# Two transformer blocks in fp32 on one core: low-part products one block later, weight conversions behind them, buffers for squares, and an earlier last split

## The reference

```python
def rms_norm(x, g):
    return x * lax.rsqrt(jnp.mean(x * x, axis=-1, keepdims=True) + EPS) * g

def first_block(x, p, ...):
    z = rms_norm(h, g_mix_pre) @ w_in            # D=1024
    ...                                          # convolution, attention, short convolution, pooling
    h = h + rms_norm(mix, g_mix_post)            # mix = concat(...) @ w_out
    ff = jnp.square(jax.nn.relu(rms_norm(h, g_mlp_pre) @ w_up)) @ w_down
    h = h + rms_norm(ff, g_mlp_post)
    gate = jax.nn.sigmoid(rms_norm(h, g_ple_pre) @ w_ple_gate)
    return h + rms_norm((p @ w_ple_proj) * gate, g_ple_post)

def second_block(x, ...):
    z = rmsnorm(x, ln_mix_g) @ w_in
    ...                                          # sliding attention, gated linear attention
    x = x + merged @ w_out
    a, u = jnp.split(rmsnorm(x, ln_ffn_g) @ w_ffn_in, 2, axis=-1)
    return x + (jax.nn.silu(causal_dwconv(a)) * u) @ w_ffn_out
```

## Time and profile before

| | us |
|---|---|
| median of 3 runs | 1488.1 |
| lowest and highest | 1486.35, 1490.41 |
| the profiled execution | 1486.49 |
| its span in the profile | 1484.7 |
| busy: TensorE, VectorE, ScalarE, GpSimd | 1454.5, 804.9, 560.2, 257.8 |
| mean granted clock of TensorE (1 is full) | 0.993 |

### The profile page before, as it was taken

One profiled execution on the slowest core, in us unless ns is written; L12 is line 12 of the kernel. 1 busy time (PEld: TensorE's weight loads), 2 busy tenths in 40 slices (PEclk: granted clock), 3 DMA queues, 4 the chain that ended last, 5 costly groups with the idle time before them and its releaser, 6 DMA issues.

```text
span 1484.7 us, 17752 instructions
## 1 busy us (share of the span) xinstructions
PE 1454.5 (98%) x6978; PEld 1188.2 (80%) x6978; DVE 804.9 (54%) x1167; ACT 560.2 (38%) x829; POOL 257.8 (17%) x170
## 2 busy tenths in 40 slices
PE   9999989999999999889999999999999999999998
PEld 7866768888888887767888888888887888888887
DVE  5688465433333347675767734734535665534554
ACT  5345434522324124442455546322224443323310
POOL 4234344301101012341033201300003000000000
PEclk9999999999999999999999999999999999999999
DMA  6221222333323332221211211233332233332331
GB/s 229 86 71 57 71 64 78 114 99 99 101 86 98 99 100 73 72 69 59 84 43 44 68 47 57 90 95 100 97 102 77 80 114 99 98 101 86 102 99 69
DMA packets 36131, 129.18 MB, mean 87 GB/s; under 512 B 4024, under 2 KB 4280, under 8 KB 36048
## 3 DMA queue, kind: packets, MB, share of 16 engines
q1 hardware_dynamic: 35760, 127.78, 27.6%
q10 hardware_dynamic: 288, 0.26, 0.1%
HBM read 125.91 MB, written 2.10 MB: 86 GB/s over the span
## 4 chain that ended last, share of the span: by engine, by line
PE 89%; DVE 5%; ACT 2%; issue 2%; POOL 1%; DMA 0%; ACTq 0%; DVEq 0%; POOLq 0%
PE P L1080 27%; PE P L1082 26%; PE P L1081 26%; PE P L1339 1%; DVE P L1893 1%; PE P L1225 1%; DVE WST L2125 1%; POOL AC L2370 1%; PE P L1121 1%; PE P L1176 1%; PE P L1301 1%; POOL DD L2370 1%; PE P L1382 0%; PE P L1322 0%; PE P L1187 0%
## 5 line engine op out<-in xcount | busy, mean ns | idle before, releaser
L1080 PE MATMUL P<-AH,WH 128*128 128x512 f32 x1104 | 444.9, 403 | 11.0 <-issue 5.0
L1082 PE MATMUL P<-AH,WL 128*128 128x512 f32 x1104 | 433.5, 393 | 0.0
L1081 PE MATMUL P<-AL,WH 128*128 128x512 f32 x1104 | 433.1, 392 | 0.0
L1419 ACT ACTIVATE WH<-WR 128x1024 fp32r<-128x1024 f32 x232 | 244.0, 1052 | 338.5 <-PE P L1082 322.6
L1739 DVE TENSOR_TENSOR WL<-WR,WH 128x1024 fp32r<-128x1024 f32 x215 | 277.1, 1289 | 148.8 <-ACT WH L1419 148.1
L1080 PEld LDWEIGHTS P<-AH,WH 128*128 128x128 f32 x1104 | 209.1, 189 | 64.4 <-issue 13.9
L1082 PEld LDWEIGHTS P<-AH,WL 128*128 128x128 f32 x1104 | 209.1, 189 | 44.8
L1081 PEld LDWEIGHTS P<-AL,WH 128*128 128x128 f32 x1104 | 209.5, 190 | 42.0 <-issue 0.7
L1080 PE MATMUL P<-FH,WH 128*128 128x512 f32 x432 | 168.0, 389 | 0.0
L1081 PE MATMUL P<-FL,WH 128*128 128x512 f32 x432 | 168.0, 389 | 0.0
L1082 PE MATMUL P<-FH,WL 128*128 128x512 f32 x432 | 168.0, 389 | 0.0
(11 more groups left out here) (323 smaller groups left out, 1867.7 us busy)
## 6 DMA issues: line engine op xcount, KB each, us to landing
WR<-in_ws SPq DMA_DIRECT2D x232, 512.0 KB, 3.6
out<-Y SPq DMA_DIRECT2D x8, 256.0 KB, 2.0
H<-in_xT SPq DMA_DIRECT2D x3, 512.0 KB, 7.8
C<-in_const SPq DMA_DIRECT2D x1, 946.5 KB, 10.6
H<-in_xT SPq DMA_DIRECT2D x2, 256.0 KB, 4.2
PR<-in_pT SPq DMA_DIRECT2D x1, 512.0 KB, 4.8
WR<-in_ws SPq DMA_DIRECT2D x1, 384.0 KB, 4.6
WR<-in_ws ACTq DMA_DIRECT2D x1, 128.0 KB, 3.8
```

Source lines behind the costliest of these rows:

```text
L1080: e.matmul(P, wh, xh, start=start, stop=False)
L1081: e.matmul(P, wh, xl, start=False, stop=False)
L1082: ins = e.matmul(P, wl, xh, start=False, stop=stop)
L1419: e.activation(m.WH[:, c % NW, :], m.WR[:, c % NRAW, :], ACT.Copy).then_inc(*at.up("w_hi", "w_hi", c))
```

## The change

It does six things. (1) In a head, the three matmuls of a block product are taken apart: `mm_hi` does `WH` with `AH` and `WL` with `AH` for block j of all tiles, then `mm_lo` does `WH` with `AL` of block j-1, so low parts lag one block; from the fourth chunk on, `ahead` is called at `mm_lo`. (2) Every head has five tiles side by side (the gate's had four), and `sums` stands in the middle of block 7. (3) In stage 5 the splits and squares of blocks 0 to 5 are said inside the loop of `mix2`. (4) At `p1` and `p3` squares 5 and 6 have buffers of their own, square 6 is added on VectorE, and one `warm` product goes. (5) The addition of `H` block 1 moves from GpSimd to VectorE. (6) The root's first guess takes one operation fewer.

```diff
@@ -312,31 +312,54 @@
             self.say("w_load", NRAW)
             make(1)
             self.say("square", s, 0, 0)
-        else:
+        elif s != "5":
             make(0)
             make(1)
             rest(0)
-        rest(1)
-        make(2)
-        got = [self.ring() for _ in range(3)] + [self.bank(b) for b in (6, 7)[:len(specs) - 4]]
+        if s != "5":
+            rest(1)
+            make(2)
+        got = [self.ring() for _ in range(3)] + [self.bank(b) for b in (6, 7)]
+        behind = []
+
+        def low(j):
+            for t, i in zip(got, behind):
+                if i // CH >= 3:
+                    self.ahead(i)
+                self.say("mm_lo", t, i, (x, j), j == 7)
         for j in range(8):
-            if j == 7:
-                self.sums(s, 0)
+            ids = []
             for m, t in enumerate(got):
-                self.block(t, specs[m][j], (x, j), j == 0, j == 7)
+                if j == 7 and m == 2:
+                    self.sums(s, 0)
+                i = len(self.plan)
+                if i // CH < 3:
+                    self.ahead(i)
+                self.plan.append(specs[m][j])
+                ids.append(i)
+                self.say("mm_hi", t, i, (x, j), j == 0)
+            if j:
+                low(j - 1)
+            behind = ids
+            if s == "5":
+                if j < 2:
+                    make(j + 6)
+                    rest(j + 6)
+                continue
             if j < 5:
                 make(j + 3)
             if j < 6:
                 rest(j + 2)
+        low(7)
         b = self.spread(s)
-        out = got + [self.tile(specs[len(got)], [(x, j) for j in range(8)])]
+        out = got + [self.tile(q, [(x, j) for j in range(8)]) for q in specs[5:]]
         self.say("rbc", s, b)
         return out
 
     def post(self, n, direct, fill=None):
 
         if fill is None:
-            self.say("warm", self.bank(6), 3)
+            self.say("warm", self.bank(6), 2)
         self.sums(n, direct)
         if fill is None:
             self.say("warm", self.bank(6), 2)
@@ -627,6 +650,10 @@
             t = self.tile([block("w_out_2", 128 * q, 128 * m) for q in range(8)], [("M2", q) for q in range(8)])
             self.say("mix2", m, t)
             self.close(t)
+            if 0 < m < 7:
+                self.say("x_hi", "5", m - 1)
+                self.say("x_lo", "5", m - 1)
+                self.say("square", "5", m - 1, 0)
         return lambda m: None
 
     def decay(self):
@@ -963,6 +990,13 @@
     def rs(self, i):
         return (self.RS, self.RT)[i // 4][:, i % 4, :]
 
+    def square(self, n, i):
+
+        SQ, AC = self.sq(n)
+        if n in ("p1", "p3") and i >= 5:
+            return SQ[:, 1, :] if i == 7 else self.post(n)[1][:, i - 5, :]
+        return AC if i == 0 else SQ[:, i % 2, :]
+
     def rbc(self, s):
         return {"1": self.RBC1, "2": self.RBC2, "3": self.RBC2, "4": self.RBC3, "5": self.RBC4}[s]
 
@@ -1080,6 +1114,31 @@
         e.matmul(P, wh, xh, start=start, stop=False)
         e.matmul(P, wh, xl, start=False, stop=False)
         ins = e.matmul(P, wl, xh, start=False, stop=stop)
+        if stop:
+            ins.then_inc(*at.up("full", "full", t.id))
+            if ends:
+                at.also(("full", t.id), "w_used", c)
+        elif ends:
+            ins.then_inc(*at.up("w_used", "w_used", c))
+
+    def mm_hi(t, i, x, start):
+
+        c, o = i // CH, (i % CH) * 128
+        P, xh = m.bank[t.bank][:], m.x(*x)[0]
+        part = int(o >= FIRST)
+        w.wait_ge(*(at("w_hi", c) if c else at("w_hi0", part)))
+        w.wait_ge(*at("x_hi", *x))
+        if start:
+            free(t)
+        e.matmul(P, m.WH[:, c % NW, o:o + 128], xh, start=start, stop=False)
+        w.wait_ge(*(at("w_lo", c) if c else at("w_lo0", part)))
+        e.matmul(P, m.WL[:, c % NW, o:o + 128], xh, start=False, stop=False)
+
+    def mm_lo(t, i, x, stop):
+
+        c, wh, wl, ends = weights(i)
+        w.wait_ge(*at("x_lo", *x))
+        ins = e.matmul(m.bank[t.bank][:], wh, m.x(*x)[1], start=False, stop=stop)
         if stop:
             ins.then_inc(*at.up("full", "full", t.id))
             if ends:
@@ -1162,7 +1221,7 @@
 
 
     def sums(n, t, direct):
-        SQ, AC = m.sq(n)
+        AC = m.sq(n)[1]
         if first[0]:
             first[0] = False
             w.wait_ge(*at("params"))
@@ -1178,7 +1237,7 @@
         if direct:
             w.wait_ge(*at("square", n, 7))
             for q in range(4):
-                ins = e.matmul(P[:, q:q + 1], SQ[:, 1, 128 * q:128 * q + 128], one, start=False, stop=True,
+                ins = e.matmul(P[:, q:q + 1], m.square(n, 7)[:, 128 * q:128 * q + 128], one, start=False, stop=True,
                                skip_group_check=True)
         ins.then_inc(*at.up("full", "full", t.id))
 
@@ -1434,11 +1493,12 @@
             *at.up("x_hi", "x_hi", "A" + s, i))
 
     def square(n, i, direct):
-        SQ, AC = m.sq(n)
         w.wait_ge(*at("summand", n, i))
-        if i >= 3:
+        if n in ("p1", "p3") and i >= 5:
+            w.wait_ge(*at("summed", n, 3))
+        elif i >= 3:
             w.wait_ge(*at("summed", n, i - 2))
-        e.activation(AC if i == 0 else SQ[:, i % 2, :], m.summed(n, i), ACT.Square).then_inc(
+        e.activation(m.square(n, i), m.summed(n, i), ACT.Square).then_inc(
             *at.up("square", "square", n, i))
 
 
@@ -1757,10 +1817,7 @@
         v, y, u = m.roots(name, n)
         e.tensor_scalar(v, ps, scale, EPS, ALU.mult, ALU.add).then_inc(*at.up("newton", "root0", name))
         w.wait_ge(*at("root0", name))
-        e.tensor_scalar(u.bitcast(I32), v.bitcast(I32), 1, None, ALU.logical_shift_right).then_inc(
-            *at.up("newton", "root1", name))
-        w.wait_ge(*at("root1", name))
-        e.tensor_scalar(y.bitcast(I32), u.bitcast(I32), -1.0, float(0x5F3759DF), ALU.mult, ALU.add).then_inc(
+        e.tensor_scalar(y.bitcast(I32), v.bitcast(I32), -0.5, float(0x5F3759DF), ALU.mult, ALU.add).then_inc(
             *at.up("newton", "root2", name))
         w.wait_ge(*at("root2", name))
         for k in range(3):
@@ -1777,6 +1834,14 @@
         rsqrt(n, m.bank[t.bank][:, 0:4], 4, 1.0 / 1024)
         at.also(("root0", n), "read", t.id)
 
+    def square(n, i, direct):
+
+        if n in ("p1", "p3") and i == 7:
+            AC = m.sq(n)[1]
+            w.wait_ge(*at("square", n, 6))
+            w.wait_ge(*at("summed", n, 5))
+            e.tensor_tensor(AC, AC, m.square(n, 6), ALU.add).then_inc(*at.up("summed_last", "summed", n, 6))
+
     def rbc(s, t):
         w.wait_ge(*at("full", t.id))
         e.tensor_copy(m.rbc(s)[:], m.bank[t.bank][:]).then_inc(*at.up("rbc", "rbc", s))
@@ -1794,7 +1859,7 @@
             *at.up("normed", "normed", n, i))
         if i == 7:
             at.also(("normed", n, 7), "read", t.id)
-        if i % 2 == 0:
+        if i % 2 == 0 or i == 1:
             w.wait_ge(*at("normed", n, i))
             e.tensor_tensor(m.H[:, i, :], m.H[:, i, :], u, ALU.add).then_inc(*at.up("h", "h", s, i))
 
@@ -2362,16 +2427,16 @@
         did("w_lo", c)
 
     def square(n, i, direct):
-        if i == 0 or i >= 8 - direct:
+        if i == 0 or i >= 8 - direct or (n in ("p1", "p3") and i == 6):
             return
-        SQ, AC = m.sq(n)
+        AC = m.sq(n)[1]
         w.wait_ge(*at("square", n, i))
         turn()
-        e.tensor_tensor(AC, AC, SQ[:, i % 2, :], ALU.add).then_inc(*at.up("summed", "summed", n, i))
+        e.tensor_tensor(AC, AC, m.square(n, i), ALU.add).then_inc(*at.up("summed", "summed", n, i))
         did("summed", n, i)
 
     def residual(n, i, t):
-        if i % 2 == 0:
+        if i % 2 == 0 or i == 1:
             return
         s = {"p1": "2", "p2": "3", "p3": "4"}[n]
         w.wait_ge(*at("normed", n, i))
```

More of the change, by code:

```diff
@@ L1401, in gn_spread @@
         spread_to(m.bank[t.bank], m.roots("gn", 16)[1][:, 4 * hh:4 * hh + 4]).then_inc(*at.up("full", "full", t.id))
-    run = {"mm": mm, "mm_tokens": mm_tokens, "mm_values": mm_values, "mm_narrow": mm_narrow, "warm_first": warm_first, "warm": warm, "sums": sums, "spread": spread,
+    run = {"mm": mm, "mm_hi": mm_hi, "mm_lo": mm_lo, "mm_tokens": mm_tokens, "mm_values": mm_values, "mm_narrow": mm_narrow, "warm_first": warm_first, "warm": warm, "sums": sums, "spread": spread,
            "scores1": scores1, "turn1": turn1, "values1": values1, "ln_mean": ln_mean, "ln_center": ln_center,
@@ L2325, in down2 @@
             e.tensor_tensor(y, y, o, ALU.add).then_inc(*at.up("y4", "y4", 2, i))
-    run = {"w_lo0": w_lo0, "w_lo": w_lo, "x_lo": x_lo, "rsqrt_norm": rsqrt_norm, "rbc": rbc, "residual": residual, "qk1": qk1,
+    run = {"w_lo0": w_lo0, "w_lo": w_lo, "x_lo": x_lo, "rsqrt_norm": rsqrt_norm, "square": square, "rbc": rbc, "residual": residual, "qk1": qk1,
            "forget_in": forget_in, "forget0": forget0, "forget2": forget2, "mask1": mask1, "scale1": scale1,
```

## The result

The changed kernel takes 1500.4 us (median of 5 runs, 1497.3 to 1501.4), the kernel before 1486.35 us on the same chip (5 runs): a ratio of 1.0091 (95% interval 1.0073 to 1.0109). It is slower by about 14 us; forecast were 1482.3 us and a range of 1474 to 1488 (from 1488.1 us, the median of three of these five runs of the kernel before).

What follows compares the result with a forecast made beforehand. TensorE, busy 1454.5 of 1484.7 us, was taken as the bound. Stages 2 and 4 +1.0, stage 3 -4.95, stage 5 -1.6, root -0.2 gave -5.8: 1480.7, plus 1.6 to the median, 1482.3 us; range 1474 to 1488.

Steps and rivals of the forecast that it cites:

- The rest: Last group of terms: -0.2 us for another root, nothing for stage 1, later weight conversions and weight loads.
- Later issue of weight conversions: Conversions in heads asked for five blocks later still have at least 9.5 us, so this costs nothing.
- my slower rival: In heads' later chunks `WL` queues behind VectorE's splits and residuals, costing TensorE 13 us: 1495 us, chance 0.05.
- The chain: Residual, `AH`, square and GpSimd addition through eight blocks; 28.9 us in stages 2 and 4, +1.5 us in stage 3.
- theory A: From the experiments: TensorE starts a head earlier but waits for the chain of squares, then works at 0.50.
- The clock: Stages 2 and 4: behind a 3.8 us wait in two pieces, a fallen stretch costs 1.0 us each, at most 1.7.
- Stage 3: Five tiles at once: +1.5 us of chain, -4.5 for 20 more products before the sums, -2.95 and +1.0 of clock: -4.95 us.
- the starts: First products of stages 2 and 4 come 2.5 us sooner, 1.5 us after the first addition into `H`.
- the root of `p1`: Boundary ahead of stage 2: with the last addition of squares on VectorE, about 0.65 us sooner.
- stage 5: With splits made inside the product loop ahead of it, the wait at its start goes: -1.6 us.
- Stage 1: Its first product needs no `AL` but then waits for `WL`; counted at nothing.
- rival 2: All given back: chain 29.5 us or more, early starts become waits with full fallen stretches; 1486.2 us, chance 0.20.

Runs made afterwards that it cites:

- e5: The changed kernel with the weight conversions asked for at the high products in all stages, as before the change: 1495.4 us, 1.0051.
- e9: The changed kernel with the weight conversions asked for at the high products in stages 2 to 4 only: 1485.6 us, 0.9996.
- e6: The changed kernel with the last square of each head summed by TensorE in place of a last addition on GpSimd: 1494.4 us, 1.0044.
- e7: The changed kernel with 4 warming products ahead of the sums of stages 2, 3 and 4: 1490.3 us, 1.0021.
- e10: e9 with the last square of heads 2 to 4 summed by TensorE and 6 warming products, not 2, at `p3`: 1478.6 us, 0.9937.
- e11: e10 with four tiles side by side in stage 3 and 4 warming products at `p3`: 1481.4 us, 0.9964.
- e2: The kernel before with only the early splits and squares of stage 5: 1485.0 us, 0.9996.
- e4: The changed kernel with 14 warming products ahead of the sums of stages 2, 3 and 4: 1514.9 us, 1.0190.

## Why the prediction was wrong

**The step that failed first** is in "The rest": "Later issue of weight conversions: ... nothing". I asked only whether `WL` would come in time for TensorE; that it did (the longest wait for `WL` in the change is 0.6 us, in stage 1), so my slower rival, conversions that fall behind, wasn't it either. What I didn't ask is what these conversions meet. In stages 2 and 4 the first two of a head moved from places where GpSimd was idle to places where it adds, the third further into an addition. The Trainium skill, page "SBUF — State Buffer", section "Who interferes with whom", says that a VectorE instruction with two SBUF inputs contends with a GpSimd instruction that reads SBUF. The trace agrees for `WL`, which reads two tensors of 128 x 1024: 2.31 us in place of 1.22. I had weighed this for `AL` alone. I applied it to the operation that was moved away from GpSimd, not to the ones moved towards it. Measured: 2.35 us on the chains of stages 2 and 4, 1.6 on that of stage 3, shown by e5 and e9.

**The chain.** Forecast 28.9 us (28 to 29.5) in stages 2 and 4, measured 29.84 and 29.83; in stage 3 1.5 us more than before, measured 30.80 against 28.06, 2.7 more. The same cause, for 1.6 of them in stage 3; the 1.1 that stay are near my 1.5. Without the moved conversions it is 27.5 us, below my range, and even so the sums wait 2.2 us: theory A stands on its own, since the chain of blocks and not TensorE sets when a head's sums come.

**The clock, the largest term.** I took 1.0 us (at most 1.7) per head for a stretch at 0.50. Measured are 6.83 us behind each wait, 7.38 us of time for what takes 4.54: 2.8 us a head, beyond my bound. The earlier trace rows held the evidence: the wait of 3.36 us was followed by 6.81 us at 0.50, those of 2.50 by 3.40, and I priced the forecast wait of 3.8 us like the shorter ones, since it comes in two pieces. It does, but the pieces are of 1.06 and 3.17 us. Here waits of 3.17 us gave 6.83 us, of 2.2 us (e9) 3.41, of 0.7 us (e6) 3.4 to 6.8. The fall also went beyond the heads: 13.64 us at 0.50 in mixer 2, 5.1 us lost where nothing was changed. It was 3.41, 6.8, 10.2 or 13.7 us there in the other kernels, with the same products. What sets its length at this place the runs don't show; e7 had 13.7 there and the trace of e10 none.

**Stage 3.** Forecast -4.95 us, measured 4.7 us more to the spread and 5.4 less behind it, -0.7, and then 2.5 more at `p3`. I left out what the root's delay does to the eight gates behind it. With four tiles it was better by 2.6 us in this kernel, with a short chain worse by 2.8 (e10 to e11, intervals that overlap).

**Right were** the starts (1.51 us after the first addition, -2.6 us at the boundary), the root of `p1` (the sums there come 0.62 us sooner; forecast 0.65), and stage 5 (-2.1 us in the change's trace, -1.9 in e2's; forecast -1.6). Stage 1, which I counted at nothing, lost 0.9 us: 0.64 of it is a wait for `WL` of an early chunk. By the new order high block 6 of stage 5 is wanted behind 85 products, not 90; nothing hangs on it.

**The sum, once more.** With the measured sizes: three heads +16.6 (waits of 3.17 and about 1.06 us, and half clock), boundary -2.6, rest of stage 3 -5.4, `p3` +2.5, mixer 2 +4.8, stage 5 -2.1, stage 1 +0.9, feed-forward 1 -0.8: 13.9 us. My rival 2 (all given back) named the mechanism, sums that wait and stretches behind them, and ended at 1486 since its clock was bounded at 1.7 us a head and mixer 2 stood at nothing.

**How much is clock in all.** Each run has its mean granted clock beside its time, and a time multiplied by it leaves out what the fallen clock adds. The kernel before took 1481.6 to 1492.9 us in 27 runs on one chip, at clocks of 0.995 to 0.989; multiplied, they lie between 1473.5 and 1476.7. So it is mostly the clock that sets the runs of one kernel apart. By the same product, an estimate, the change (1500.4 us at 0.985) lost 22.5 us to the clock and the kernel before (1486.5 at 0.993) 10.4: 12 of the 14 us between them.

**What stays open:** why the clock fell for 13.64 us in mixer 2, and so 5 of the 14 us are shown as lost there but not explained; and why a stretch is longer behind one wait than behind another of the same length (e6: 3.4 and 6.8 us behind waits of 0.7).

## What to carry to other kernels

An early start of the engine that bounds a kernel is worth only what the next thing that it waits for allows: find the chain behind the sum, the root or the reduction first, and shorten that one (here the last addition handed to TensorE, and the conversions back where they were). When a step is moved in a queue, ask not only whether its result is in time but what runs on the neighbour engine at its new place. A wait that a fall of the clock follows costs more than its length; if it can't be removed, a few products without use in it were the cheapest repair here (10 us for 12 instructions, e7).

## What the runs showed of the hardware

A conversion to `WL` (128 x 1024) on VectorE takes 1.22 us alone and 2.31 us when a GpSimd addition of 1.36 us that began 0.12 us earlier runs beside it (221.37 and 221.25 in the change): it ends 1.07 us after that addition, as if little of its work were done by then. An fp32 product of 128 x 512 takes 0.86 us (14 of them 12.0 us in e4), against 0.227 for an fp32r one. The length of a stretch at 0.50 (1.2 GHz) differed by kernel at the same place of the program and with the same work: none in the trace of e10, 3.41 us in that of the kernel before, 13.7 in those of the change and of e7, all in mixer 2.
